# Dense products that read their columns and write their outputs two and two from the halves of a tile

## The chip, the cores and the metric

One core of a Trainium2 chip runs the whole kernel. The metric is the device time of one launch in microseconds; lower is better. TensorE does the matrix products into PSUM (8 banks of 512 fp32 a partition), ScalarE (ACT) and VectorE (DVE) prepare operands and take results out, the SyncE queue (SP) loads from HBM.

## What is computed

One inference step of a decoder layer for 256 prompt tokens and 8 sequences of 8 sample tokens, 320 token columns in all. The reference, cut to what matters here:

```python
h = rms_norm(x, norm_mix_pre[l])
u = h @ w_in[l]                       # 2048 -> 11264: recurrence, attention and gate columns
...
y_hg = o_hg.reshape(b, L, HG_WIDTH) @ w_branch_hg[l]      # 1024 -> 2048
y_da = o_da.reshape(b, L, DA_WIDTH) @ w_branch_da[l]      # 1024 -> 2048
mixed = (jax.nn.sigmoid(g_hg) * y_hg + jax.nn.sigmoid(g_da) * y_da) @ w_out[l]   # 2048 -> 2048
x = x + rms_norm(mixed, norm_mix_post[l])
h = rms_norm(x, norm_ffn_pre[l])
gate, up = jnp.split(h @ w_ffn_up[l], 2, axis=-1)         # 2048 -> 2 * 5632
ffn = (jax.nn.silu(gate) * up) @ w_ffn_down[l]            # 5632 -> 2048
x = x + rms_norm(ffn, norm_ffn_post[l])
```

Between them lie a gated linear recurrence (HGRN2) and differential attention; the sample tokens also attend to a paged cache of 2048 past tokens for each sequence. Everything is float32.

## The kernel before

All activations are kept transposed: 128 features on the partitions, the 320 tokens (T) along the free dimension, contiguous. A weight "granule" is 128 x 1024 floats (512 KB), loaded by the SP queue into one of 12 (later 8) `raw` slots. Each float is split in two parts of the reduced float32 type F32R (written fp32r in the profile): ACT writes the high part `w_hi`, DVE the rest `w_lo`; activations are split in the same way (`x_hi`/`x_lo`, `h2_hi`/`h2_lo`, `m_hi`/`m_lo`, `br_hi`/`br_lo`, `hid_hi`/`hid_lo`). A product is then the sum of three: high by high, low by high and high by low. So a granule is eight 128 x 128 weight blocks, each used in three matmuls of 320 columns: 24 matmuls, each with its own weight load, adding up in PSUM columns 0 to 319 of a bank (`ps[:, bank, 0:T]`).

These "dense products" are written in seven places: `products` (L410 to L412: input projection, branches, output projection, most of the up projection), `half_products` (L421, the first weight set), `pe_last_set` (L1371 to L1373), `up_half` (L1462) and `pe_first_hidden` (L1493 to L1497), `down_granule` (L1818 to L1820) and `down_end` (L1836 to L1838). The program of each engine is an order written out by hand with semaphores between the engines: `granule_used` lets ACT write the next `w_hi`, `hi_ready` and `lo_ready` lead on to DVE and TensorE; nothing is reordered by a scheduler.

Other matmuls stand among them: attention scores of a cache page group (L912: four products of 32 output rows and 512 columns side by side, read as 4 runs of 128), the values (L947, 256 columns), sums of squares in F32R (L932, L933: 320 and 256 columns), transposes and, at the end, the addition of x by an identity in plain float32 (L1850, L1869: 320 columns).

The stages in order: input projection sets, then eight rounds (one head of the recurrence and attention and one sample sequence each, with 16 dense granules), to about 900 us; branches and output projection; up projection from about 1090 us; down projection to the end.

Of the kernel before, what the change touches and what calls it, by code (L numbers as in the profile page):

```python
# [29 lines left out]
T = SEQ + NB * NQ  # L30
# [11 lines left out]
RAW, HALVES = 8, 4  # L42
# [78 lines left out]
def build(nc, xT, ck, cv, st, pt, w_in, w_hg, w_da, w_out, w_up, w_dn, nrm, hgw, lbl, lamv,  # L121
          table, c_ident, c_scan, c_causal, c_own, c_pick, c_hot, c_coef,
          y_T, k_T, v_T, h_p, h_s):
    with ExitStack() as ctx:
# [12 lines left out]
        w_hi = [sb(f"w_hi{j}", [P, 1024], F32R) for j in range(HALVES)]  # L137
        w_lo = [sb(f"w_lo{j}", [P, 1024], F32R) for j in range(HALVES)]
# [15 lines left out]
        ps = ctx.enter_context(nc.psum_tensor("ps", [P, 8, 512], F32))  # L154
# [95 lines left out]
        m_hi = sb("m_hi", [P, KT, T], F32R, at_branch)  # L250
        m_lo = sb("m_lo", [P, KT, T], F32R, at_branch)
# [11 lines left out]
        h2_hi = sb("h2_hi", [P, KT, T], F32R)  # L263
# [130 lines left out]
        def round_lo(dve, r, kind, q):  # L394

            d = 8 * FIRST + 16 * r + (8 if kind == "D" else 0) + q
            split_lo(dve, d, ring_of(r).slot[kind, q], q)

        def products(pe, r, slot, xh, xl, bank, q, nq, free, by_bank=True):

            pe.wait_ge(lo_ready, r + 1)
            wh = w_hi[slot % HALVES][:, :].rearrange("p (c m k) -> p c m k", c=2, m=4)
            wl = w_lo[slot % HALVES][:, :].rearrange("p (c m k) -> p c m k", c=2, m=4)
            for m in range(4):
                if q == 0:
                    free(m)
                out = ps[:, bank + m, 0:T]
                for c in range(2):
                    first, last = q == 0 and c == 0, q == nq - 1 and c == 1
                    pe.matmul(out, wh[:, c, m, :], xh(c), start=first, stop=False)  # L410
                    pe.matmul(out, wl[:, c, m, :], xh(c), start=False, stop=False)  # L411
                    mm = pe.matmul(out, wh[:, c, m, :], xl(c), start=False, stop=last)  # L412
                if by_bank and q == nq - 1 and m < 3:
                    mm.then_inc(set_done, 1)
            mm.then_inc(granule_used, 1)

        def half_products(pe, w, x, bank, first, last):

            for m in range(4):
                for c in range(2):  # L420
                    mm = pe.matmul(ps[:, bank + m, 0:T], w.rearrange("p (c m k) -> p c m k", c=2, m=4)[:, c, m, :], x(c),  # L421
                                   start=first and c == 0, stop=last and c == 1)
                if last and bank == 0 and m < 3:
                    mm.then_inc(set_done, 1)
            return mm
# [933 lines left out]
        def pe_last_set(pe):  # L1359

            s = BLOCKS - 1
            pe_out_set(pe, s, upto=8 - TOGETHER)
            qs = range(8 - TOGETHER, 8)
            pe.wait_ge(lo_ready, R_OUT + 8 * s + 8)
            for m in range(4):
                for q in qs:
                    wh = w_hi[q % HALVES][:, :].rearrange("p (c m k) -> p c m k", c=2, m=4)
                    wl = w_lo[q % HALVES][:, :].rearrange("p (c m k) -> p c m k", c=2, m=4)
                    for c in range(2):
                        k, last = 2 * q + c, q == 7 and c == 1  # L1370
                        pe.matmul(ps[:, m, 0:T], wh[:, c, m, :], m_hi[:, k, :], start=False, stop=False)  # L1371
                        pe.matmul(ps[:, m, 0:T], wl[:, c, m, :], m_hi[:, k, :], start=False, stop=False)
                        mm = pe.matmul(ps[:, m, 0:T], wh[:, c, m, :], m_lo[:, k, :], start=False, stop=last)  # L1373
                    if m == 3:
                        mm.then_inc(granule_used, 1)
                if m < 3:
                    mm.then_inc(set_done, 1)
# [79 lines left out]
        def up_half(pe, w, x, q, part, first, last):  # L1457

            w4 = w.rearrange("p (c m k) -> p c m k", c=2, m=4)
            for m in range(4):  # L1460
                for c in range(2):
                    mm = pe.matmul(ps[:, 4 * part + m, 0:T], w4[:, c, m, :], x[:, 2 * q + c, :],  # L1462
                                   start=first and c == 0, stop=last and c == 1)
            return mm

# [21 lines left out]
        def pe_first_hidden(pe):  # L1487
            pe.wait_ge(lo_ready, R_UP + 1)
            wh, wl = (w[0][:, :].rearrange("p (c m k) -> p c m k", c=2, m=4) for w in (w_hi, w_lo))
            for c in range(2):  # L1490
                pe.wait_ge(e_act.sem, e_act.at(0, "h0" if c else "ha"))
                for m in range(4):
                    pe.matmul(ps[:, m, 0:T], wh[:, c, m, :], h2_hi[:, c, :], start=c == 0, stop=False)  # L1493
                    pe.matmul(ps[:, m, 0:T], wl[:, c, m, :], h2_hi[:, c, :], start=False, stop=False)
                pe.wait_ge(e_vec.sem, e_vec.at(0, "l0" if c else "la"))
                for m in range(4):
                    mm = pe.matmul(ps[:, m, 0:T], wh[:, c, m, :], h2_lo[:, c, :], start=False, stop=False)  # L1497
            mm.then_inc(granule_used, 1)
            for i, (q, part) in enumerate(FIRST_UP):
                if i == 0:  # L1500
                    continue
                if i == 1:
                    pe.wait_ge(e_act.sem, e_act.at(0, "rs"))
                pe.wait_ge(lo_ready, R_UP + i + 1)
                pe.wait_ge(e_act.sem, e_act.at(0, f"h{q}"))
                wh, wl = w_hi[i % HALVES][:, :], w_lo[i % HALVES][:, :]
                up_half(pe, wh, h2_hi, q, part, q == 0, False)
                up_half(pe, wl, h2_hi, q, part, False, False)
                pe.wait_ge(e_vec.sem, e_vec.at(0, f"l{q}"))
                up_half(pe, wh, h2_lo, q, part, False, q == 7).then_inc(granule_used, 1)  # L1510
                if i == GATE_END:

                    pe.wait_ge(e_vec.sem, e_vec.at(0, "sum"))
                    for e in range(2):
                        own = slice(T // 2 * e, T // 2 * e + T // 2)
                        ins = pe.matmul(ps[:, e, T:T + T // 2], ones[:, :], squares[:, 0, own], start=True, stop=True)
                    e_pe2.done(ins, "ss")
# [270 lines left out]
        def pe_rest(pe):  # L1788
# [18 lines left out]
            def down_granule(pas, k, r, slot, use, q):  # L1807
                pe.wait_ge(lo_ready, r + 1)
                wh, wl = w_hi[slot % HALVES], w_lo[slot % HALVES]
                xh, xl = hid_hi[slot % HALVES][:, :], hid_lo[slot % HALVES][:, :]  # L1810
                for m in range(8):
                    if pas and q == 0:
                        pe.wait_ge(g_act.sem, g_act.at(0, f"c{m}"))
                    if not pas and q == 0 and m in (0, 4):
                        pe.wait_ge(f_vec.sem, f_vec.at(HB - 1, "u" if m else "g"))
                    c = slice(P * m, P * m + P)
                    add = dict(start=False, stop=q > 3, skip_group_check=q > 3)
                    pe.matmul(ps[:, m, 0:T], wh[:, c], xh, **dict(add, start=q == 0))  # L1818
                    pe.matmul(ps[:, m, 0:T], wl[:, c], xh, **add)  # L1819
                    ins = pe.matmul(ps[:, m, 0:T], wh[:, c], xl, **dict(add, stop=q >= 3))  # L1820
                    if q == 11 and m < 7:
                        ins.then_inc(down_done, 1)
                ins.then_inc(granule_used, 1)

            def down_end(pas, k, r, slot, use, q):

                if q < 11:
                    return
                pe.wait_ge(lo_ready, r + 1)
                for m in range(8):  # L1830
                    c = slice(P * m, P * m + P)
                    for back in range(MERGED - 1, -1, -1):
                        at = (slot - back) % HALVES
                        xh, xl = hid_hi[at][:, :], hid_lo[at][:, :]
                        add = dict(start=False, stop=True, skip_group_check=True)
                        pe.matmul(ps[:, m, 0:T], w_hi[at][:, c], xh, **add)  # L1836
                        pe.matmul(ps[:, m, 0:T], w_lo[at][:, c], xh, **add)
                        ins = pe.matmul(ps[:, m, 0:T], w_hi[at][:, c], xl, **add)  # L1838
                        if m == 7:
                            ins.then_inc(granule_used, 1)  # L1840
                    if m < 7:
                        ins.then_inc(down_done, 1)
# [349 lines left out]
```

## Time and profile before

| what | value |
|---|---|
| median of 2 runs | 2034.06 us (2033.51 to 2034.61) |
| the profiled execution's own time | 2033.87 us |
| its span, first to last instruction | 2032.3 us |
| TensorE busy | 2022.9 us, 14806 matmuls |
| VectorE / ScalarE busy | 1047.4 / 826.5 us |
| HBM traffic over the span | 219 GB/s |

The span is what the views below divide; 1.6 us of the execution's time lie outside it. A matmul's row begins when it begins to read, and its end is modelled, so rows overlap: the time from one start to the next, or the number of starts in a stretch, tells what a matmul costs. The clock that TensorE is granted is given as a share of 2.4 GHz.

### The profile page before, as it was taken

To read this page: it belongs to the slowest core of one execution; us is meant where nothing else is said; L and a number is where in the kernel's file an instruction comes from. 1 tells how busy PE (TensorE), PEld (TensorE's weight loads), DVE (VectorE), ACT (ScalarE), POOL (GpSimd) and SP (SyncE) were. 2 spreads that over 40 slices of the span, in tenths; PEclk is the share of its full clock that TensorE was granted. 3 is DMA by queue.
4 is the path that set the end of the run, shared out by engine and by line. 5 is a ranking of instruction groups with operands and counts; after the bars stand their busy time and mean duration, and the time that the engine had idled before them with its cause. 6 is when DMAs were issued, how large, how long until landed. Compare 5 with 4: busy or idle time off the path is not lost.

```text
span 2032.3 us, 38356 instructions
## 1 busy us (share of the span) xinstructions
PE 2022.9 (100%) x14806; PEld 1912.6 (94%) x14806; DVE 1047.4 (52%) x1340; ACT 826.5 (41%) x1099; POOL 74.7 (4%) x119
## 2 busy tenths in 40 slices
PE   9999999999999999999999999999999999999999
PEld 9999888888888888899999999999999999999998
DVE  7443555646556465565547644444444445445445
ACT  6333443434435354354345433333333333435344
POOL 1001010000100000000000000000000000000000
PEclk9999999999999999999999999999999999999999
DMA  8767888988889888876544444445444454444441
GB/s 304 163 230 241 301 335 316 357 306 335 336 315 354 314 332 332 328 277 229 172 143 137 152 149 148 141 145 165 145 152 142 141 164 145 148 151 146 155 144 52
DMA packets 123982, 444.13 MB, mean 219 GB/s; under 512 B 14581, under 2 KB 18709, under 8 KB 123856
## 3 DMA queue, kind: packets, MB, share of 16 engines
q1 hardware_dynamic: 112720, 402.31, 55.5%
q0 software_dynamic: 9968, 39.48, 6.5%
q10 hardware_dynamic: 1232, 1.47, 0.2%
q8 instruction: 43, 0.70, 0.1%
q14 instruction: 19, 0.16, 0.0%
HBM read 423.28 MB, written 22.54 MB: 219 GB/s over the span
## 4 chain that ended last, share of the span: by engine, by line
PE 98%; DMA 1%; DVE 1%; ACT 0%; issue 0%; SPq 0%; DVEq 0%
PE ps L410 23%; PE ps L411 22%; PE ps L412 22%; PE ps L1818 5%; PE ps L1820 5%; PE ps L1819 5%; PE ps L912 3%; PE ps L947 3%; PE ps L1462 3%; PE ps L421 1%; PE ps L921 1%; DMA gates<-uT 0%; DMA raw<-w_hg 0%; PE ps L733 0%; PE ps L720 0%; PE ps L481 0%
## 5 line engine op out<-in xcount | busy, mean ns | idle before, releaser
L369 DVE TENSOR_TENSOR w_lo<-raw,w_hi 128x1024 fp32r<-128x1024 f32 x416 | 505.1, 1223 | 539.5 <-ACT w_hi L364 286.7
L410 PE MATMUL ps<-x_hi,w_hi 128*128 128x320 f32 x1472 | 464.4, 316 | 0.0
L411 PE MATMUL ps<-x_hi,w_lo 128*128 128x320 f32 x1472 | 454.8, 309 | 0.0
L364 ACT ACTIVATE w_hi<-raw 128x1024 fp32r<-128x1024 f32 x236 | 247.9, 1062 | 422.5 <-PE ps L412 395.7
L412 PE MATMUL ps<-x_lo,w_hi 128*128 128x320 f32 x1344 | 415.2, 309 | 0.0
L410 PE MATMUL ps<-h_hi,w_hi 128*128 128x320 f32 x1280 | 395.8, 309 | 0.0
L411 PE MATMUL ps<-h_hi,w_lo 128*128 128x320 f32 x1280 | 395.8, 309 | 0.0
L412 PE MATMUL ps<-h_lo,w_hi 128*128 128x320 f32 x1280 | 395.8, 309 | 0.0
L410 PEld LDWEIGHTS ps<-x_hi,w_hi 128*128 128x128 f32 x1472 | 276.5, 188 | 36.1 <-issue 29.2
L411 PEld LDWEIGHTS ps<-x_hi,w_lo 128*128 128x128 f32 x1472 | 276.7, 188 | 0.1
L412 PEld LDWEIGHTS ps<-x_lo,w_hi 128*128 128x128 f32 x1344 | 252.5, 188 | 0.0
L410 PEld LDWEIGHTS ps<-h_hi,w_hi 128*128 128x128 f32 x1280 | 240.4, 188 | 0.0
L411 PEld LDWEIGHTS ps<-h_hi,w_lo 128*128 128x128 f32 x1280 | 240.4, 188 | 0.0
L412 PEld LDWEIGHTS ps<-h_lo,w_hi 128*128 128x128 f32 x1280 | 240.4, 188 | 0.0
L1818 PE MATMUL ps<-hid_hi,w_hi 128*128 128x320 f32 x680 | 210.1, 309 | 0.0
L1820 PE MATMUL ps<-hid_lo,w_hi 128*128 128x320 f32 x680 | 210.0, 309 | 0.0
L1819 PE MATMUL ps<-hid_hi,w_lo 128*128 128x320 f32 x680 | 210.0, 309 | 0.0
L392 ACT ACTIVATE w_hi<-raw 128x1024 fp32r<-128x1024 f32 x124 | 130.0, 1054 | 109.3 <-DMA raw<-w_in 97.1
L1818 PEld LDWEIGHTS ps<-hid_hi,w_hi 128*128 128x128 f32 x680 | 127.7, 188 | 0.1
L1819 PEld LDWEIGHTS ps<-hid_hi,w_lo 128*128 128x128 f32 x680 | 127.7, 188 | 0.0
L1820 PEld LDWEIGHTS ps<-hid_lo,w_hi 128*128 128x128 f32 x680 | 127.7, 188 | 0.0
L1760 DVE TENSOR_TENSOR hid_lo<-hidden,hid_hi 128x320 fp32r<-128x320 f32 x88 | 43.3, 492 | 154.5 <-ACT w_hi L1667 154.1
(330 smaller groups left out, 2375.0 us busy)
## 6 DMA issues: line engine op xcount, KB each, us to landing
raw<-w_in SPq DMA_DIRECT2D x176, 512.0 KB, 6.4
raw<-w_up SPq DMA_DIRECT2D x176, 512.0 KB, 3.5
raw<-ck SPq DMA_DIRECT2D x128, 512.0 KB, 6.2
raw<-cv SPq DMA_DIRECT2D x128, 512.0 KB, 6.9
raw<-w_dn SPq DMA_DIRECT2D x88, 512.0 KB, 3.5
raw<-w_out SPq DMA_DIRECT2D x32, 512.0 KB, 3.7
uT<-stage POOLq DMA_DIRECT2D x14, 640.0 KB, 3.9
raw<-w_hg SPq DMA_DIRECT2D x16, 512.0 KB, 4.6
```

Source lines behind the costliest of these rows:

```text
L364: act.activation(w_hi[slot % HALVES][:, :], raw[slot][:, :], ACT.Copy).then_inc(hi_ready, 1)
L369: dve.tensor_tensor(w_lo[half][:, :], raw[slot][:, :], w_hi[half][:, :].bitcast(F32), ALU.subtract).then_inc(lo_ready, 1)
L392: act.activation(w_hi[q % HALVES][:, :], raw[ring_of(r).slot[kind, q]][:, :], ACT.Copy).then_inc(hi_ready, 1)
L410: pe.matmul(out, wh[:, c, m, :], xh(c), start=first, stop=False)
L411: pe.matmul(out, wl[:, c, m, :], xh(c), start=False, stop=False)
L412: mm = pe.matmul(out, wh[:, c, m, :], xl(c), start=False, stop=last)
L912: ins = pe.matmul(ps[32 * j:32 * j + 32, 7, :], q_rows[:, h, :], raw_all[:, at:at + QUAD, h * PAGE:(h + 1) * PAGE], start=e == 0, stop=e == 1)
L947: ins = pe.matmul(ps[32 * j:32 * j + 32, 6, 0:2 * DV], p_keys[:, p, 32 * j:32 * j + 32], raw[slot][:, 2 * DV * j:2 * DV * (j + 1)], start= ...
L1462: mm = pe.matmul(ps[:, 4 * part + m, 0:T], w4[:, c, m, :], x[:, 2 * q + c, :], start=first and c == 0, stop=last and c == 1)
L1818: pe.matmul(ps[:, m, 0:T], wh[:, c], xh, **dict(add, start=q == 0))
L1819: pe.matmul(ps[:, m, 0:T], wl[:, c], xh, **add)
L1820: ins = pe.matmul(ps[:, m, 0:T], wh[:, c], xl, **dict(add, stop=q >= 3))
```

## The change

A helper `paired` splits the 320 columns of a tile into two halves of 160 and each half into 80 pairs, and walks them in the order: pair 0 of the first half, pair 0 of the second, pair 1 of the first, and so on (columns 0, 1, 160, 161, 2, 3, 162, 163, ...). Every dense product reads its moving operand in this order and writes its PSUM output in the same order, so that each column lands where it did. No tile is stored differently, and the weights are read as before. The built program has as many instructions on each engine as before, in the same order; only the form of these matmuls is now 128x80x2x2 in place of 128x320. The other matmuls are left alone. All lines below the helper move down by 4.

```diff
+        def paired(cols):
+
+            return cols.rearrange("p (a b c) -> p b a c", a=2, c=2)
+
         def products(pe, r, slot, xh, xl, bank, q, nq, free, by_bank=True):
...
-                out = ps[:, bank + m, 0:T]
+                out = paired(ps[:, bank + m, 0:T])
                 for c in range(2):
                     first, last = q == 0 and c == 0, q == nq - 1 and c == 1
-                    pe.matmul(out, wh[:, c, m, :], xh(c), start=first, stop=False)
-                    pe.matmul(out, wl[:, c, m, :], xh(c), start=False, stop=False)
-                    mm = pe.matmul(out, wh[:, c, m, :], xl(c), start=False, stop=last)
+                    pe.matmul(out, wh[:, c, m, :], paired(xh(c)), start=first, stop=False)
+                    pe.matmul(out, wl[:, c, m, :], paired(xh(c)), start=False, stop=False)
+                    mm = pe.matmul(out, wh[:, c, m, :], paired(xl(c)), start=False, stop=last)
...
-                xh, xl = hid_hi[slot % HALVES][:, :], hid_lo[slot % HALVES][:, :]
+                xh, xl = paired(hid_hi[slot % HALVES][:, :]), paired(hid_lo[slot % HALVES][:, :])
...
-                    pe.matmul(ps[:, m, 0:T], wh[:, c], xh, **dict(add, start=q == 0))
-                    pe.matmul(ps[:, m, 0:T], wl[:, c], xh, **add)
-                    ins = pe.matmul(ps[:, m, 0:T], wh[:, c], xl, **dict(add, stop=q >= 3))
+                    pe.matmul(paired(ps[:, m, 0:T]), wh[:, c], xh, **dict(add, start=q == 0))
+                    pe.matmul(paired(ps[:, m, 0:T]), wl[:, c], xh, **add)
+                    ins = pe.matmul(paired(ps[:, m, 0:T]), wh[:, c], xl, **dict(add, stop=q >= 3))
```

The other five places are edited in the same way.

## Rows read from the trace of the kernel before

**Rows 1.** The page: busy time by engine, and the granted clock in 40 slices.

```profile
PE 2022.9 (100%) x14806; PEld 1912.6 (94%) x14806; DVE 1047.4 (52%) x1340; ACT 826.5 (41%) x1099; POOL 74.7 (4%) x119
...
PEclk9999999999999999999999999999999999999999
```

**Rows 2.** The page: the chain that ended last, by engine.

```profile
PE 98%; DMA 1%; DVE 1%; ACT 0%; issue 0%; SPq 0%; DVEq 0%
```

**Rows 3.** Waits of TensorE: us in total, times, longest.

```profile
PE ps L481 <- DVE ones L1956: 1.8, 1, 1.8
PE ps L960 <- ACT o_rows L831: 1.2, 1, 1.2
```

**Rows 4.** The page: loads of the weights by tensor, with their count.

```profile
raw<-w_in SPq DMA_DIRECT2D x176, 512.0 KB, 6.4
raw<-w_up SPq DMA_DIRECT2D x176, 512.0 KB, 3.5
...
raw<-w_dn SPq DMA_DIRECT2D x88, 512.0 KB, 3.5
raw<-w_out SPq DMA_DIRECT2D x32, 512.0 KB, 3.7
...
raw<-w_hg SPq DMA_DIRECT2D x16, 512.0 KB, 4.6
raw<-w_da SPq DMA_DIRECT2D x16, 512.0 KB, 8.4
```

**Rows 5.** Stretches: busy time and starts (x) of each engine, clock, DMA share, GB/s.

```profile
core 0: us, PE busy (x) PEld busy (x) DVE busy (x) ACT busy (x) POOL busy (x), PEclk, DMA share, GB/s
1300.00:1900.00 600.00, 600.00 (x4092) 599.91 (x4091) 277.37 (x261) 215.39 (x246) 0.00 (x0) 1.00 0.45 149
...
100.00:200.00 100.00, 100.00 (x686) 99.93 (x685) 39.67 (x40) 31.51 (x33) 9.39 (x15) 1.00 0.66 226
...
250.00:350.00 100.00, 100.00 (x814) 85.32 (x813) 56.31 (x102) 44.45 (x70) 9.09 (x14) 1.00 0.88 329
```

**Rows 6.** Timeline at 277 us: start us, duration us, instruction.

```profile
277.20 0.30 PE L932 MATMUL ps<-sq_hi,ones_r 128*128 128x320 f32 x1
277.20 0.19 PEld L933 LDWEIGHTS ps<-sq_lo,ones_r 128*128 128x128 f32 x1
277.34 0.31 PE L933 MATMUL ps<-sq_lo,ones_r 128*128 128x320 f32 x1
277.34 0.19 PEld L932 LDWEIGHTS ps<-sq_hi,ones_r 128*128 128x128 f32 x1
277.49 0.28 PE L932 MATMUL ps<-sq_hi,ones_r 128*128 128x256 f32 x1
277.49 0.19 PEld L933 LDWEIGHTS ps<-sq_lo,ones_r 128*128 128x128 f32 x1
277.61 0.28 PE L933 MATMUL ps<-sq_lo,ones_r 128*128 128x256 f32 x1
```

**Rows 7.** Timeline at 2021 us: plain float32 additions by an identity.

```profile
2021.60 2.59 PE L1869 MATMUL ps<-ffn,ident 128*128 128x320 f32 x9
```

**Rows 8.** Timeline at 216 us: page scores, four groups of four matmuls.

```profile
216.40 1.92 PE L912 MATMUL ps<-raw,q_rows 128*32 128x512 f32 x16
```

**Rows 9.** Groups by line and shape: xcount, busy us, mean ns of one.

```profile
L912 PE MATMUL ps<-raw,q_rows 128*32 128x512 f32 x512 | 61.6, 598 | 0.0
...
L1869 PE MATMUL ps<-ffn,ident 128*128 128x320 f32 x18 | 5.3, 432 | 0.0
```

**Rows 10.** The page: the two splits of a weight granule.

```profile
L369 DVE TENSOR_TENSOR w_lo<-raw,w_hi 128x1024 fp32r<-128x1024 f32 x416 | 505.1, 1223 | 539.5 <-ACT w_hi L364 286.7
...
L364 ACT ACTIVATE w_hi<-raw 128x1024 fp32r<-128x1024 f32 x236 | 247.9, 1062 | 422.5 <-PE ps L412 395.7
```

More of the change, by code:

```diff
@@ L420, in half_products @@
                 for c in range(2):
-                    mm = pe.matmul(ps[:, bank + m, 0:T], w.rearrange("p (c m k) -> p c m k", c=2, m=4)[:, c, m, :], x(c),
-                                   start=first and c == 0, stop=last and c == 1)
+                    mm = pe.matmul(paired(ps[:, bank + m, 0:T]), w.rearrange("p (c m k) -> p c m k", c=2, m=4)[:, c, m, :],
+                                   paired(x(c)), start=first and c == 0, stop=last and c == 1)
                 if last and bank == 0 and m < 3:
@@ L1370, in pe_last_set @@
                         k, last = 2 * q + c, q == 7 and c == 1
-                        pe.matmul(ps[:, m, 0:T], wh[:, c, m, :], m_hi[:, k, :], start=False, stop=False)
-                        pe.matmul(ps[:, m, 0:T], wl[:, c, m, :], m_hi[:, k, :], start=False, stop=False)
-                        mm = pe.matmul(ps[:, m, 0:T], wh[:, c, m, :], m_lo[:, k, :], start=False, stop=last)
+                        pe.matmul(paired(ps[:, m, 0:T]), wh[:, c, m, :], paired(m_hi[:, k, :]), start=False, stop=False)
+                        pe.matmul(paired(ps[:, m, 0:T]), wl[:, c, m, :], paired(m_hi[:, k, :]), start=False, stop=False)
+                        mm = pe.matmul(paired(ps[:, m, 0:T]), wh[:, c, m, :], paired(m_lo[:, k, :]), start=False, stop=last)
                     if m == 3:
@@ L1461, in up_half @@
                 for c in range(2):
-                    mm = pe.matmul(ps[:, 4 * part + m, 0:T], w4[:, c, m, :], x[:, 2 * q + c, :],
+                    mm = pe.matmul(paired(ps[:, 4 * part + m, 0:T]), w4[:, c, m, :], paired(x[:, 2 * q + c, :]),
                                    start=first and c == 0, stop=last and c == 1)
@@ L1492, in pe_first_hidden @@
                 for m in range(4):
-                    pe.matmul(ps[:, m, 0:T], wh[:, c, m, :], h2_hi[:, c, :], start=c == 0, stop=False)
-                    pe.matmul(ps[:, m, 0:T], wl[:, c, m, :], h2_hi[:, c, :], start=False, stop=False)
+                    pe.matmul(paired(ps[:, m, 0:T]), wh[:, c, m, :], paired(h2_hi[:, c, :]), start=c == 0, stop=False)
+                    pe.matmul(paired(ps[:, m, 0:T]), wl[:, c, m, :], paired(h2_hi[:, c, :]), start=False, stop=False)
                 pe.wait_ge(e_vec.sem, e_vec.at(0, "l0" if c else "la"))
                 for m in range(4):
-                    mm = pe.matmul(ps[:, m, 0:T], wh[:, c, m, :], h2_lo[:, c, :], start=False, stop=False)
+                    mm = pe.matmul(paired(ps[:, m, 0:T]), wh[:, c, m, :], paired(h2_lo[:, c, :]), start=False, stop=False)
             mm.then_inc(granule_used, 1)
@@ L1833, in down_end @@
                         at = (slot - back) % HALVES
-                        xh, xl = hid_hi[at][:, :], hid_lo[at][:, :]
+                        xh, xl = paired(hid_hi[at][:, :]), paired(hid_lo[at][:, :])
                         add = dict(start=False, stop=True, skip_group_check=True)
-                        pe.matmul(ps[:, m, 0:T], w_hi[at][:, c], xh, **add)
-                        pe.matmul(ps[:, m, 0:T], w_lo[at][:, c], xh, **add)
-                        ins = pe.matmul(ps[:, m, 0:T], w_hi[at][:, c], xl, **add)
+                        pe.matmul(paired(ps[:, m, 0:T]), w_hi[at][:, c], xh, **add)
+                        pe.matmul(paired(ps[:, m, 0:T]), w_lo[at][:, c], xh, **add)
+                        ins = pe.matmul(paired(ps[:, m, 0:T]), w_hi[at][:, c], xl, **add)
                         if m == 7:
```

## The prediction

> **What bounds the kernel now.** I read the page first, from the top. TensorE is busy for 2022.9 of 2032.3 us at the full granted clock, which is 2.4 GHz [rows 1], and the chain that ended last is TensorE for 98% [rows 2]. The view of waits says the same from the other side: the longest waits of TensorE are single ones of 1.8 and 1.2 us [rows 3]. So the kernel is one queue of matmuls, and whatever changes the time of a dense matmul changes the end by that, times the number of them. Since rows of matmuls overlap and their ends are modelled, their durations (0.31 us) say nothing here. I count starts. From 1300 to 1900 us, where nothing but dense products runs, there are 4092 starts in 600 us: 600 / 4092 = 146.6 ns each [rows 5]. This step is the same where the DMA engines are at 0.45 and where they are at 0.66 (686 starts in 100 us, 145.8 ns) [rows 5], so memory traffic does not set it.
>
> **How many there are.** The weights come in 176 + 176 + 88 + 32 + 16 + 16 = 504 granules [rows 4], each of 24 matmuls: 12,096. At 146.6 ns that is 1773 us of the 2032.3 us. All of them are changed; the other 2710 of the 14806 are not.
>
> **What the 146.6 ns are made of.** At 2.4 GHz, 320 columns at one a clock would take 133.3 ns. Two neighbours tell what lies above. The sums of squares at 277 us have the same type: the step from one start to the next is 0.14 to 0.15 us after 320 columns and 0.12 us after 256 [rows 6]. So 64 columns are worth about 0.027 us, close to one a clock (26.7 ns), and the time goes with the columns. Each of these also has its own weight load of 128 columns, and one of them was over in time for a step of 0.12 us; a weight load is not what holds the dense step at 0.147 us. The second neighbour is plain float32 at the end: nine matmuls of 320 columns take 2.59 us from the first start to the last end, one lasts 0.432 us, so a step is (2.59 - 0.432) / 8 = 0.270 us [rows 7, 9]. That is two clocks a column (266.7 ns) and 3.3 ns over. With those 3.3 ns as the cost of beginning a matmul, an F32R one of 320 columns should take 136.6 ns. It takes 10.0 ns more, which no row explains. Twelve thousand times 10.0 ns are 121 us: this is all that a better walk over the columns could win.
>
> **The change part by part.**
>
> Instructions, waits, loads, evacuations: nothing is added, removed or moved; each matmul is still one instruction with one weight load, and its output lands in the same columns, so ACT and DVE read banks as before. Cost 0.
>
> The moving operand is read as pairs of 4-byte elements, 8 bytes, with a jump of 640 bytes forward or back between pairs: 160 pairs and 159 jumps. The trace of before has no matmul that reads so. The nearest rows: the page scores read 512 columns as four runs of 128, with three jumps. Sixteen of them, in four groups of four that run side by side, take 1.92 us to the last end, one lasts 0.598 us [rows 8, 9], so a group's step is (1.92 - 0.598) / 3 = 0.441 us at most, where 512 columns at two clocks and the start cost would be 430 ns. Three jumps cost at most 11 ns together, and probably less, since the four of a group begin a little apart. This excludes an expensive jump, not a cheap one: 159 jumps at 11 / 3 ns would be 583 ns, far more than the other bound. So the bounds are taken thus. From below: the 10.0 ns vanish, -10.0 x 12,096 = -121 us. From above: the columns go at the rate of plain float32, (270 - 146.6) x 12,096 = +1493 us.
>
> The output is written in the same order, 8 bytes to a place. Its bounds are the same two, and it shares them with the read, since both go column by column in one stream.
>
> I take 0 for both. The row that it is nearest to is the dense step itself: at 2.4 GHz one column a clock is a stream that is most easily delivered as two 4-byte elements at a time, and a walk that keeps pairs together asks for as many pairs as before. The steps at 277 us [rows 6], with a slope of one clock a column, fit a stream with no refetch cost that a jump could multiply.
>
> A rule bears on this. The Trainium skill, page "Advanced Engine Details and Errata", section "Memory Cachelines", says that PSUM has lines of two fp32 values, SBUF lines of 16 bytes that want at least two hits each, and that "every two consecutive elements should be contiguous for best throughput": by that the change costs nothing, since each pair fills a PSUM line and hits an SBUF line twice. The same section says that any non-contiguous access pattern significantly slows down matmuls; by that the time would be that of the second rival below. No row of this trace shows either, because no matmul in it hops within 128 columns. The Trainium skill's page "Vector Engine (DVE) Microarchitecture Reference", section "Measured stream behaviour on trn2", gives for VectorE 1.065 ns a column with all streams hopping in aligned pairs against 1.054 contiguous; if TensorE did alike, an estimate is 1% of 1773 us, 18 us, which is inside no change. No run here shows that.
>
> Sum: 2033.87 us (the profiled execution's own time, 0.2 us under the median of 2034.06) + 0 = 2034 us. If it is off by a nanosecond a matmul either way it moves by 12 us, so this case by itself reaches from 2015 to 2060.
>
> **The rivals.**
>
> *The 10 ns go (faster).* If the unexplained 10.0 ns are a clash between neighbouring columns of one tile, say a PSUM column that is read to be added to while the last one is written, taking turns between two halves could separate them. For it: the excess is there in F32R and missing in plain float32, which asks for half as much in a time. Against it: the same clash would show in the slope, and from 256 to 320 columns the slope looks like one clock. Time: 2034 - 121 = 1913 us. The other engines would follow: a granule would take 24 x 136.6 = 3.28 us against 1.223 us of DVE and 1.062 us of ACT for its splits [rows 10]; in the rounds the DMA engines, now at 0.88 [rows 5], would be asked for about 5% more, 0.92.
>
> *Each hop costs a fetch (slower).* If the excess is the price of going from one 16-byte run of four floats to the next, 80 times a matmul, the paired walk does that 160 times and pays it twice: +10.0 ns, or +13.3 ns if the 3.3 ns belong to it too. Time: 2034 + 121 = 2155 to 2034 + 161 = 2195 us. It decides from the first matmul, as nothing hides TensorE. For it: an excess of 10 ns over 80 runs is a plausible 0.13 ns each. Against: again the slope.
>
> *The stream falls to half rate (much slower).* If full rate needs long contiguous runs, in the operand or in PSUM, the dense step becomes that of plain float32, 270 ns: 2034 + 1493 = 3527 us. For it: the trace shows only two rates, and nothing in it shows full rate without contiguity; scores with jumps run at the slower one already, and can't tell. Against: nothing but the pairs themselves.
>
> *The change does nothing*, because the walk is put back in order when built. The form of the instruction in the built program (128x80x2x2) speaks against it; its time is that of the forecast and it is counted there.
>
> **How the numbers follow.** No change 0.50 (2015 to 2060 us); the excess goes, in part or whole, 0.14 (1913 us); each hop costs a fetch 0.15 (2155 to 2195 us); half rate or thereabouts 0.21 (3527 us). The range from 1910 to 2200 us holds the first three, 0.79, and leaves out the last. Two per cent, 41 us or 3.4 ns a dense matmul, is about what a measurement of this kernel can tell from no change. Faster by more than that 0.13, within it 0.51, slower 0.36.
>
> **What would show it.** In the profile after, the count of starts from 1300 to 1900 us decides at once: 4092 for no change, about 4390 for the first rival, 3750 to 3830 for the second, 2220 for the third. In the second and third the weight loads would no longer be busy throughout, the splits of ACT and DVE would stand in longer idle times, and GB/s would fall with them. The steps of L932 and L933 must stay at 0.15 and 0.12 us in every case, and the granted clock at full. The forecast is wrong if TensorE's walk over three dimensions has a price of its own, or if pairs are not the unit in which SBUF or PSUM serve it.

## The result and the profile after

The changed kernel takes 2763.55 us (2 runs, 2763.49 to 2763.61) against 2034.06 us: a ratio of 1.3585, 95% interval 1.3552 to 1.3617. That is 729.5 us more.

The page of the kernel after, busy time by engine, granted clock, and the chain that ended last:

```profile
PE 2753.8 (100%) x14806; PEld 2490.7 (90%) x14806; DVE 1051.8 (38%) x1340; ACT 826.0 (30%) x1099; POOL 74.5 (3%) x119
...
PEclk9999999999999999999999999999999999999999
...
PE 99%; DVE 0%; DMA 0%; ACT 0%; issue 0%; SPq 0%; DVEq 0%
```

The counts and the clock are those of [rows 1, 2], and the work of DVE and ACT is the same to within half a per cent: the same instructions, TensorE hardly ever waiting, and all of the time gone into its matmuls. The stretches of the kernel after show the dense step (columns: stretch, busy time and starts of each engine, clock, DMA share, GB/s):

```profile
1800.00:2400.00 600.00, 600.00 (x2905) 566.13 (x2904) 194.36 (x170) 142.98 (x149) 0.00 (x0) 1.00 0.33 107
```

Against 4092 starts in [rows 5] there are 2905: 600 / 2905 = 206.5 ns a matmul. Times 12,096, the 59.9 ns more are 725 us of the 729.5. The waits of TensorE stay single and small, and the split of a weight granule on DVE takes as long as in [rows 10] with more idle time in front of it (waits, then the group on the page):

```profile
PE ps L485 <- DVE ones L1960: 1.8, 1, 1.8
PE ps L964 <- ACT o_rows L835: 0.6, 1, 0.6
```

```profile
L369 DVE TENSOR_TENSOR w_lo<-raw,w_hi 128x1024 fp32r<-128x1024 f32 x416 | 506.9, 1224 | 866.5 <-ACT w_hi L364 534.3
```

Matmuls that were not changed kept their time. The sums of squares, of the same type and read in plain order in the midst of the slower ones, still step by 0.15 us after 320 columns and 0.12 us after 256, as in [rows 6]. The additions by an identity at the end do too: from 2753.64 to 2754.72 us four records, 0.270 us each, as in [rows 7].

```profile
378.24 0.32 PE L936 MATMUL ps<-sq_hi,ones_r 128*128 128x320 f32 x1
378.39 0.31 PE L937 MATMUL ps<-sq_lo,ones_r 128*128 128x320 f32 x1
378.54 0.28 PE L936 MATMUL ps<-sq_hi,ones_r 128*128 128x256 f32 x1
378.66 0.28 PE L937 MATMUL ps<-sq_lo,ones_r 128*128 128x256 f32 x1
...
2753.64 1.24 PE L1854 MATMUL ps<-o_all,ident 128*128 128x320 f32 x4
2754.72 1.24 PE L1873 MATMUL ps<-ffn,ident 128*128 128x320 f32 x4
```

### The profile page after: what moved, and what is told of

It is laid out like the page before. It is cut to its first block, busy times and chain, and to the rows that moved or that the text cites. A ratio compares the mean times of both kernels' runs of the same rounds, so it can differ in the third digit from the quotient of the medians.

```text
span 2761.9 us, 38356 instructions
## 1 busy us (share of the span) xinstructions
PE 2753.8 (100%) x14806; PEld 2490.7 (90%) x14806; DVE 1051.8 (38%) x1340; ACT 826.0 (30%) x1099; POOL 74.5 (3%) x119
## 4 chain that ended last, share of the span: by engine, by line
PE 99%; DVE 0%; DMA 0%; ACT 0%; issue 0%; SPq 0%; DVEq 0%
PE ps L414 24%; PE ps L415 23%; PE ps L416 23%; PE ps L1824 5%; PE ps L1822 5%; PE ps L1823 5%; PE ps L1466 3%; PE ps L916 2%; PE ps L951 2%; PE ps L425 1%; PE ps L925 1%; PE ps L737 0%; PE ps L724 0%; DVE ffn L1784 0%; PE ps L697 0%; PE ps L674 0%
## 5 line engine op out<-in xcount | busy, mean ns | idle before, releaser
L414 PE MATMUL ps<-x_hi,w_hi 128*128 128x320 f32 x1472 | 566.5, 385 | 0.0
L415 PE MATMUL ps<-x_hi,w_lo 128*128 128x320 f32 x1472 | 558.1, 379 | 0.0
L416 PE MATMUL ps<-x_lo,w_hi 128*128 128x320 f32 x1344 | 509.5, 379 | 0.0
L414 PE MATMUL ps<-h_hi,w_hi 128*128 128x320 f32 x1280 | 492.8, 385 | 0.0
L415 PE MATMUL ps<-h_hi,w_lo 128*128 128x320 f32 x1280 | 492.8, 385 | 0.0
L416 PE MATMUL ps<-h_lo,w_hi 128*128 128x320 f32 x1280 | 492.8, 385 | 0.0
L414 PEld LDWEIGHTS ps<-x_hi,w_hi 128*128 128x128 f32 x1472 | 286.2, 194 | 54.3 <-issue 35.0
L1822 PE MATMUL ps<-hid_hi,w_hi 128*128 128x320 f32 x680 | 261.8, 385 | 0.0
L1823 PE MATMUL ps<-hid_hi,w_lo 128*128 128x320 f32 x680 | 261.8, 385 | 0.0
L1824 PE MATMUL ps<-hid_lo,w_hi 128*128 128x320 f32 x680 | 261.8, 385 | 0.0
```

Of the source, the lines that this page charges most:

```text
L414: pe.matmul(out, wh[:, c, m, :], paired(xh(c)), start=first, stop=False)
L415: pe.matmul(out, wl[:, c, m, :], paired(xh(c)), start=False, stop=False)
L416: mm = pe.matmul(out, wh[:, c, m, :], paired(xl(c)), start=False, stop=last)
L1822: pe.matmul(paired(ps[:, m, 0:T]), wh[:, c], xh, **dict(add, start=q == 0))
L1823: pe.matmul(paired(ps[:, m, 0:T]), wl[:, c], xh, **add)
L1824: ins = pe.matmul(paired(ps[:, m, 0:T]), wh[:, c], xl, **dict(add, stop=q >= 3))
```

## The experiments

### Is it the read or the write?

Two kernels each do one half of the change.

```diff
 # e1_read_pairs: against the kernel after
-                out = paired(ps[:, bank + m, 0:T])
+                out = ps[:, bank + m, 0:T]
...
 # e2_write_pairs: against the kernel after
-                    pe.matmul(out, wh[:, c, m, :], paired(xh(c)), start=first, stop=False)
+                    pe.matmul(out, wh[:, c, m, :], xh(c), start=first, stop=False)
```

> The dense products read their moving columns two and two from the halves, but write their outputs in plain order (the columns of the output are then permuted: the result is not the reference's). The changed kernel takes 2763.6 us, a dense step of 206.5 ns against 146.6. Theory W (PSUM writes in pairs are what costs): the step stays at about 147 ns and the time at 2034 us. Theory R (the operand's reads in pairs cost): 206 ns and about 2763 us. Theory B (each costs and they add up): a step in between, about 176 ns, 2390 us.

> The dense products read their moving columns in plain order and write their outputs two and two to the halves (output columns permuted, not the reference's). Theory W: a step of about 206 ns, 2763 us. Theory R: 147 ns, 2034 us. Theory B: in between, about 176 ns, 2390 us.

Reading alone takes 2766.74 us, writing alone 2033.49 us (one run each), beside 2033.77 us for the kernel before. The stretches, first of e1_read_pairs, then of e2_write_pairs:

```profile
1800.00:2400.00 600.00, 600.00 (x2905) 566.13 (x2904) 197.28 (x171) 142.73 (x149) 0.00 (x0) 1.00 0.31 107
```

```profile
1300.00:1900.00 600.00, 600.00 (x4092) 599.91 (x4092) 277.49 (x261) 215.16 (x247) 0.00 (x0) 1.00 0.44 149
```

The counts of starts are those of after and of before, to the last one. Theory R holds: the whole loss is in the read of the moving operand, and writing PSUM in pairs is free.

### What does a hop cost?

e3_runs4 takes four columns from each half in turn, and does the whole computation.

```diff
-            return cols.rearrange("p (a b c) -> p b a c", a=2, c=2)
+            return cols.rearrange("p (a b c) -> p b a c", a=2, c=4)
```

> The walk takes four columns from each half in turn instead of two (80 runs in place of 160), reads and writes both. If the 60 ns are paid per hop (0.38 ns each), 30 ns remain: step 176.5 ns, about 2399 us. If what costs is leaving a 16-byte run before it is used up, runs of four on 16-byte boundaries cost nothing: step 147 ns, 2034 us. If any pattern of three dimensions goes at the slower rate, 206 ns, 2763 us.

It takes 2112.68 us, 1.0389 of before (1.0372 to 1.0406). The stretch from 1350 to 1950 us:

```profile
1350.00:1950.00 600.00, 600.00 (x3915) 599.98 (x3914) 265.86 (x248) 206.34 (x232) 0.00 (x0) 1.00 0.42 142
```

The step is 600 / 3915 = 153.3 ns, 6.7 above plain. Half the hops cost a ninth of the loss. So the price is not one per hop (176 was expected of that), and nearly all of it goes when a run fills 16 bytes, though not all.

### The walk by itself

e4_probe is the kernel before with sets of 16 extra matmuls behind its last one, each set another walk; what they compute is thrown away.

```python
def walk(cols, a, c):
    return cols.rearrange("p (a b c) -> p b a c", a=a, c=c)
...
for i in range(16):
    pe.matmul(acc(), wt(i), walk(hx[:, 0:T], 2, 1), start=True, stop=True)
```

> The kernel before with 36 sets of extra matmuls behind its last one (16 each, the first 64 to keep the clock up), F32R, 320 columns unless said, output to one bank, each set on a line of its own; only their steps are read, the time is that of before plus some 90 us. Plain order: Theory of a fixed cost: step = N / 2.4 + 13 ns at N = 128 to 512; theory of a cost by column: 0.458 ns x N. Read pairs: 206 ns by theory R, 147 by W; write pairs the other way round. Runs of 4, 8, 16: per hop 176, 161, 154 ns; by 16-byte runs 147 for all. Pairs with jumps of 16 bytes to 1280 bytes: all alike if a hop costs whatever its length; the 16-byte one cheaper if lines of memory are kept. Single columns (read only): about 267 ns if a fetch serves two columns. Pairs from an odd column: slower than even ones if fetches are 8 bytes. Plain float32 in pairs: 270 ns as in plain order if only the full rate is hurt.

Rows of its timeline (start us, us to the last end, line, xcount). A step is the start of the next row less that of this one, divided by 16:

```profile
2036.69 2.51 PE L1888 MATMUL ps<-w_lo,w_hi 128*128 128x320 f32 x16
2039.04 3.62 PE L1890 MATMUL ps<-w_lo,w_hi 128*128 128x320 f32 x16
2042.48 2.51 PE L1892 MATMUL ps<-w_lo,w_hi 128*128 128x320 f32 x16
2044.82 3.59 PE L1894 MATMUL ps<-w_lo,w_hi 128*128 128x320 f32 x16
2048.25 2.62 PE L1896 MATMUL ps<-w_lo,w_hi 128*128 128x320 f32 x16
...
2065.16 2.33 PE L1910 MATMUL ps<-w_lo,w_hi 128*128 128x320 f32 x16
2067.33 3.50 PE L1912 MATMUL ps<-w_lo,w_hi 128*128 128x320 f32 x16
2070.66 4.71 PE L1914 MATMUL ps<-w_lo,w_hi 128*128 128x320 f32 x16
2075.18 4.82 PE L1916 MATMUL ps<-w_lo,w_hi 128*128 128x320 f32 x16
...
2105.04 1.90 PE L1934 MATMUL ps<-w_lo,w_hi 128*128 128x128 f32 x16
2106.78 1.98 PE L1936 MATMUL ps<-w_lo,w_hi 128*128 128x192 f32 x16
2108.59 2.09 PE L1938 MATMUL ps<-w_lo,w_hi 128*128 128x256 f32 x16
2110.52 2.94 PE L1940 MATMUL ps<-w_lo,w_hi 128*128 128x384 f32 x16
2113.30 3.46 PE L1942 MATMUL ps<-w_lo,w_hi 128*128 128x448 f32 x16
2116.60 3.84 PE L1944 MATMUL ps<-w_lo,w_hi 128*128 128x512 f32 x16
```

| walk of e4_probe (320 columns, read unless said) | line | step ns |
|---|---|---|
| plain | L1888 | (2039.04 - 2036.69) / 16 = 146.9 |
| pairs from the halves: read / write / both | L1890, L1892, L1894 | 215 / 146 / 214 |
| runs of 4 from the halves: read / write / both | L1896, L1898, L1900 | 154 / 146 / 153 |
| runs of 8, of 16, both | L1906, L1908 | 153, 151 |
| **single columns from the halves** | L1910 | **(2067.33 - 2065.16) / 16 = 135.6** |
| pairs from the halves, from an odd column | L1912 | 208 |
| pairs from 80, 40, 20, 10, 5 streams | L1914 to L1922 | 271 to 290 |
| the same five, written | L1924 to L1932 | 146 to 150 |
| plain, 128 / 192 / 256 / 384 / 448 / 512 columns | L1934 to L1944 | 109 / 113 / 121 / 174 / 206 / 229 |
| one weight block for all; two banks in turn; adding up | L1946 to L1950 | 146 to 147 |

A step taken so holds the passage from one set to the next, which moves the mean of a set by a few ns beside a set of another rate, and by more beside plain float32: in e8_probe3 256 columns in singles (L1926) come out at 131 ns behind such a set and in e5_probe2 at 113.

Three things stand there. Writes by pairs or longer runs cost next to nothing in any order: eight orders written took 146 to 150 ns. At 128 and 192 columns the step is some 110 ns however few the columns. The load of 128 weight columns, which all of them have, is the likely reason, but no run varied it; at 320 columns the step is above that floor. And reading single columns in turn from the two halves, the one walk that I had held to be worse still (267 ns in the expectation), is 11 ns **faster than plain order**.

### Is that a chance of one tile?

> The kernel before with 50 sets of 16 extra matmuls (after 64 to keep the clock up) behind its last one, outputs in plain order; only their steps are read. In the first such run a read in plain order took a step of 146.6 ns, pairs from the halves 216, pairs with jumps of 16 to 256 bytes 271 to 290, single columns from the halves 135.8. Theory L (what costs is that reads close together in time fall on the same part of memory, and two streams far apart avoid it): singles stay at 136 for every distance of the two streams but a few that are multiples of a large power of two, whatever the tile and its offset; four or eight streams also 136. Theory S (135.8 is a chance of that one tile and distance): the steps scatter between 136 and 290 with distance, offset and tile. Read with a step of two columns in one stream: 136 by L if neighbours clash, 146 or more if whole lines count. By count of columns, singles: N / 2.4 + 2.5 ns for 256 and up; 112 ns below, where the weight load is the longer. If the weight load were what disturbs the plain read, one and the same weight block would give another step than two in turn (it gave 146.6 both).

Rows of its timeline: L1890 is the first of eleven sets of single columns from two streams 160 to 511 columns apart, L1912 the first of eight of pairs, at 160 to 320.

```profile
2039.11 2.33 PE L1890 MATMUL ps<-w_lo,w_hi 128*128 128x320 f32 x16
...
2063.02 3.58 PE L1912 MATMUL ps<-w_lo,w_hi 128*128 128x320 f32 x16
...
2089.53 2.59 PE L1928 MATMUL ps<-w_lo,w_hi 128*128 128x320 f32 x16
...
2126.64 4.70 PE L1960 MATMUL ps<-w_lo,w_hi 128*128 128x320 f32 x16
2131.15 4.71 PE L1962 MATMUL ps<-w_lo,w_hi 128*128 128x320 f32 x16
2135.68 2.91 PE L1964 MATMUL ps<-w_lo,w_hi 128*128 128x320 f32 x16
2138.43 4.54 PE L1966 MATMUL ps<-w_lo,w_hi 128*128 128x320 f32 x16
```

The eleven sets: (2063.02 - 2039.11) / 176 = 135.9 ns each, whatever the distance; the eight of pairs (2089.53 - 2063.02) / 128 = 207 ns. Singles begun at columns 1, 2, 4, 8 and 64, and on two other tiles, are at 136 too (plain: 146 to 148 there, 152 from column 1). One stream with a step of two columns takes (2131.15 - 2126.64) / 16 = 282 ns, four streams of single columns 172 ns, eight 272 ns. By count, singles take 163 ns for 384 columns, 189 for 448 and 216 for 512: one clock of 2.4 GHz a column and 2 to 3 ns. So theory S falls, and so does theory L, by which four and eight streams should have been at 136.

Plain float32 behaves otherwise: a record takes 269 ns in plain order (e4_probe L1952), (9.13 - 0.441) / 31 = 280 ns in pairs (L1954) and (11.00 - 0.502) / 31 = 339 ns in singles (e5_probe2 L1986), each from the first start to the last end less one record. These sets show something that I had missed in [rows 7, 9]: 16 plain float32 matmuls stand in the trace as x32. One is two records, 538 ns in all, so my upper bound took half of such a matmul for a whole one. It was no bound either: read in single columns from sixteen streams, an F32R matmul takes 311 ns (e5_probe2 L1968).

### The gain on the whole kernel

e7_read_singles changes the read alone (outputs are then permuted); e6_singles does the whole computation, and keeps the split tiles so that the reads come in the natural order of tokens (in one place two DVE instructions become four).

```diff
 # e6_singles: against the kernel before
+        def in_turn(kept):
+
+            return kept.rearrange("p (a b) -> p b a", a=2)
+
+        def kept_as(tile):
+
+            return tile.rearrange("p (a b) -> p a b", a=2) if len(tile.shape) == 2 else tile.rearrange("p n (a b) -> p n a b", a=2)
+
+        def split_of(tokens):
+
+            return tokens.rearrange("p (b a) -> p a b", a=2) if len(tokens.shape) == 2 else tokens.rearrange("p n (b a) -> p n a b", a=2)
...
-                    pe.matmul(out, wh[:, c, m, :], xh(c), start=first, stop=False)
+                    pe.matmul(out, wh[:, c, m, :], in_turn(xh(c)), start=first, stop=False)
...
-                    ins = act.activation(x_hi[:, g, :], x_raw[:, g, :], ACT.Copy, scale=nrm_w[:, 0, g:g + 1])
+                    ins = act.activation(kept_as(x_hi[:, g, :]), split_of(x_raw[:, g, :]), ACT.Copy, scale=nrm_w[:, 0, g:g + 1])
```

> All dense products of the kernel read their columns one and one from the halves (0, 160, 1, 161, ...), tiles stored as they are, outputs written in plain order (so the output columns are permuted, not the reference's). If the 135.8 ns of the extra matmuls hold for every operand tile, the step falls by 10.8 ns, 12,096 times: 131 us, 1903 us, unless the loads of the rounds or the splits become the bound, which would leave some 1930 to 1960 us. If it was a chance of that tile: between 2034 and 2760 us, with steps that differ by tile.

> The whole computation with that read: each split operand tile is kept with its even tokens in the first half and its odd tokens in the second (the ACT and DVE instructions that write high and low parts read their source with a step of two columns), and the dense products read one and one from the halves, so that they see the tokens in their natural order and write plain outputs. If the readers of e7 gain, this gains as much, 1903 us, less what slower ACT and DVE writers add where they lie on the path: at most the first set and the start of the up projection, some 5 to 10 us. If reading with a step of two slowed ACT or DVE by half in the down projection (one activation and one subtraction of 320 columns a granule, 0.5 us each), a granule would still need under 2.5 us of 3.26 us, and nothing is lost.

e7_read_singles takes 1906.62 us (0.9372 of before, 0.9357 to 0.9388), e6_singles 1906.84 us (0.9375, 0.9359 to 0.9391), beside 2033.99 us. The stretches of e6_singles, up projection and a round, and one of its groups:

```profile
1250.00:1850.00 600.00, 600.00 (x4418) 599.80 (x4417) 298.84 (x295) 239.53 (x281) 0.00 (x0) 1.00 0.47 160
250.00:350.00 100.00, 100.00 (x922) 82.84 (x921) 54.50 (x91) 43.31 (x68) 6.35 (x10) 1.00 0.91 343
```

```profile
L1680 ACT ACTIVATE hid_hi<-hidden 128x320 fp32r x72 | 36.6, 509 | 126.4 <-PE ps L1834 126.4
```

The step is 600 / 4418 = 135.8 ns; (146.6 - 135.8) x 12,096 = 131 us, of which 127 came out. In the round the DMA engines went from 0.88 [rows 5] to 0.91 and did not stop it. ACT's high part of the hidden tile, now with a step of two columns in its source, takes 509 ns where it took 472 in the kernel before, beside a granule of 24 x 135.8 = 3.26 us; e6_singles is no slower for it than e7_read_singles. TensorE now waits for a weight split, as it never did in the kernel before, 0.9 us in all:

```profile
PE ps L422 <- DVE w_lo L369: 0.9, 3, 0.3
```

### What the walk has to keep

> The kernel before with 22 more sets of 16 extra matmuls behind its last one, outputs plain; only their steps are read. Known so far (320 columns, F32R): plain 146.6 ns; two streams read column by column in turn 135.8 at every distance from 160 columns up; four such streams 170, eight 273; one stream with a step of two or three columns 283; pairs in turn from two streams 206 to 217, from five or more 271 to 290. Theory D (it is the distance of two successive reads that counts, near ones clash): two streams at 2, 4 or 8 columns inside a block read slower than 136 and only far ones reach it; the same column twice in turn, and one column 320 times, would be the worst. Theory T (each of two alternating read slots fetches ahead for its own stream and holds a piece of it, so two streams are served well wherever they are, and fetches count by the fresh pieces that they need): 135.8 at all distances from 8 columns up; two streams each with a step of two columns waste half of each piece and go to some 200 to 280; the same column twice is at 136 or less. Runs of 16, 32 and 80 from the halves: 151, 149 and 147 (towards plain). Pairs from four streams are slower than from two (206), runs of four from four streams about like from two (153) by a cost per 16-byte piece.

Rows of its timeline: L1890 reads two streams 2 columns apart in turn (0, 2, 1, 3, 4, 6, ...), L1892 to L1900 4, 8, 16, 32 and 80 columns apart, L1902 each of 160 columns twice, L1904 one column 320 times, L1906 two streams each with a step of two columns:

```profile
2038.81 2.51 PE L1890 MATMUL ps<-w_lo,w_hi 128*128 128x320 f32 x16
2041.16 2.33 PE L1892 MATMUL ps<-w_lo,w_hi 128*128 128x320 f32 x16
...
2052.02 2.34 PE L1902 MATMUL ps<-w_lo,w_hi 128*128 128x320 f32 x16
2054.20 2.38 PE L1904 MATMUL ps<-w_lo,w_hi 128*128 128x320 f32 x16
2056.41 2.50 PE L1906 MATMUL ps<-w_lo,w_hi 128*128 128x320 f32 x16
2058.75 2.61 PE L1908 MATMUL ps<-w_lo,w_hi 128*128 128x320 f32 x16
...
2073.60 2.46 PE L1918 MATMUL ps<-w_lo,w_hi 128*128 128x320 f32 x16
2075.90 2.63 PE L1920 MATMUL ps<-w_lo,w_hi 128*128 128x320 f32 x16
```

At 2 columns apart the step is 146.9 ns, from 4 up (2052.02 - 2041.16) / 80 = 135.8, each column twice 136, one column 138, two streams with a step of two 146. Theory D (near reads clash) falls: the nearest reads of all are among the fastest. Theory T fell too where it gave two spaced streams 200 to 280 ns. The other sets of the run: read in runs of 16, 32 and 80 from the halves 153, 149 and 147 ns; pairs from four streams 274 ns; runs of four from four streams (L1918) (2075.90 - 2073.60) / 16 = 144 ns, less than plain order, where about the 153 of two streams was expected, and from eight streams 154 ns.

A third one, theory P, fits most of them, and the next run tries it on walks not yet seen. It does not fit walks in which one of its readers goes back and forth between pieces that it has begun: by its rule pairs from the two halves and single columns from four streams should both take 283 ns, and they took 207 and 172.

> The kernel before with 11 more sets of 16 extra matmuls behind its last one, outputs plain; only their steps are read. Theory P, made from the sets so far: the reads of a matmul go by turns to two readers, the first takes reads 1, 3, 5, ..., the second 2, 4, 6, ..., and what counts is how many reads in a row a reader makes in one aligned piece of four columns (16 bytes): 4 or more, 135.8 ns; 2, 146.7 ns; 1, 283 ns (0.885 ns a column). Rival C (a piece costs by how often the walk as a whole goes to another one: 80 times in plain order, 320 in turns). The sets: two streams with a step of 3 columns: P 1.33 a piece, about 220 ns; with a step of 4 columns, 256 of them: P 227 ns. One stream with a step of 2, 256 columns: 227 ns by both. Every second column read twice: P 146.7. Every fourth column read twice: P 283, C about 200 (160 pieces, as pairs). Two pieces in turn column by column, then two left out: P 135.8. Runs of four from the halves, but from column 2 on, so that each run lies on two pieces: P 1 read a piece and reader, 206 to 283, against 153 when aligned. Runs of eight from column 2: P about 180 to 210. Runs of four, the second stream one column off: P between 153 and 283, since one of the readers crosses pieces.

Its timeline:

```profile
2041.42 3.58 PE L1892 MATMUL ps<-w_lo,w_hi 128*128 128x320 f32 x16
2044.83 3.85 PE L1894 MATMUL ps<-w_lo,w_hi 128*128 128x256 f32 x16
2048.50 3.86 PE L1896 MATMUL ps<-w_lo,w_hi 128*128 128x256 f32 x16
2052.18 2.52 PE L1898 MATMUL ps<-w_lo,w_hi 128*128 128x320 f32 x16
2054.54 4.73 PE L1900 MATMUL ps<-w_lo,w_hi 128*128 128x320 f32 x16
2059.09 2.36 PE L1902 MATMUL ps<-w_lo,w_hi 128*128 128x320 f32 x16
2061.29 3.51 PE L1904 MATMUL ps<-w_lo,w_hi 128*128 128x320 f32 x16
2064.63 3.68 PE L1906 MATMUL ps<-w_lo,w_hi 128*128 128x320 f32 x16
2068.14 3.47 PE L1908 MATMUL ps<-w_lo,w_hi 128*128 128x320 f32 x16
```

| walk | line | P | measured ns |
|---|---|---|---|
| two streams, step 3 | L1892 | 220 | 213 |
| two streams, step 4, 256 columns | L1894 | 227 | 229 |
| one stream, step 2, 256 columns | L1896 | 227 | 230 |
| every second column twice | L1898 | 146.7 | 147.5 |
| every fourth column twice | L1900 | 283 (rival C: 200) | 284 |
| two pieces in turn, two left out | L1902 | 135.8 | 137.5 |
| runs of 4 from column 2 | L1904 | 206 to 283 | 209 |
| runs of 8 from column 2 | L1906 | 180 to 210 | 219 |
| runs of 4, second stream one column off | L1908 | 153 to 283 | 206 |

The six sets for which P gave one number came within 4% of it, and rival C is out by 84 ns on the one that told the two apart. Of the three for which P gave only a range, two of them wide, two fell inside and the third is 9 ns above.

## Why the prediction was wrong

**The bound** was right: TensorE alone sets the end, and 12,096 times the change of a step gave 725 of 729.5 us. So were the unchanged rest, and the cover of the other engines.

**The step that failed** is "I take 0 for both", and in it the reason that "a walk that keeps pairs together asks for as many pairs as before". For the write it holds: e2_write_pairs stayed at 146.6 ns a step. For the read it does not: its term is 59.9 ns a matmul, 725 us, in place of 0. The unit is not a pair of neighbours in time. By theory P the odd reads and the even reads go two ways, and each way wants to stay in one aligned piece of four columns. In plain order each makes two reads a piece (0 and 2; 1 and 3), to which P puts down the 10 ns over one clock a column. In the paired walk one of them reads 0, 160, 2, 162 and the other 1, 161, 3, 163: each read is in another piece than the one before. The pairs, whole in time, are torn apart on both ways. What the runs show of this without the theory: pairs kept whole in the same two places took 206.5 ns where single columns took 135.8 and aligned runs of four 153, so a pair is not what the read is served by; and one stream with a step of two columns took 282 ns where two such streams in turn, with as many pieces and two reads in each, took 146. The size of the loss P does not give: its rule says 283 ns for the paired walk. A cost between the two rates was not among my cases: between the second rival's 2195 us and the third's 3527 us I had put nothing. The prediction's last sentence did name two signs of its being wrong. A walk over three dimensions with a price of its own is not it: writing by one is free, and reading by one in runs of four costs 6.7 ns. Pairs not being the unit in which SBUF serves the read is.

**The lower bound** of -121 us was a true size for a thing that this change does not do: the 10 ns can go, 127 us of them did in e6_singles, by a walk that is the changed one with runs of one in place of two (135.8 ns, where the prediction had 136.6 for a matmul without them). My first rival looked for their cause in PSUM; e7_read_singles, which changes the read alone and takes 1906.62 us, puts it in the read.

**The argument from the slope** misled me. I read one clock a column off a single step of 0.12 us at 256 columns [rows 6] and concluded that there was no cost by the piece. The extra sets give 121 ns at 256 columns and 229 at 512, 0.42 ns a column, against (216 - 163) / 128 = 0.41 for singles from 384 to 512. But plain order does not go by one line: the difference between the two walks is 8 ns at 256 columns, 9 at 288, 11 at 320 and 384, 17 at 448 and 13 at 512. It grows with the columns, unevenly, and a single step read to 10 ns, at 256 columns near the floor of some 110 ns, could not show that. It hid a mechanism that changes with the walk, and only changing the walk could show it.

**The second rival** (each hop to another run of 16 bytes costs a fetch) had the right sign. It counts 80 hops for plain order, 160 for the paired walk and 80 again for the runs of four of e3_runs4, which lost only 6.7 ns. Its price was wrong: 10.0 to 13.3 ns for the 80 more, where 59.9 were lost. And so was its count, by the walk as a whole: single columns from the halves go to another run 320 times and are the fastest walk of all, at 135.8 ns.

**The rule of the Trainium skill** that I weighed, page "Advanced Engine Details and Errata", section "Memory Cachelines": in PSUM two consecutive elements contiguous for best throughput, in SBUF at least two hits on a line of 16 bytes. The measurement decides against the second as a promise of full speed for F32R reads: pairs on 16-byte lines took 206.5 ns, plain order 146.6, and 135.8 came with single columns in turn, by P four reads on a line by each way. What it says of 16 bytes agrees with the runs of four that lost all but 6.7 ns when aligned (153) and fell back to 209 when begun two columns later. Its sentence that non-contiguous patterns slow matmuls is, for PSUM writes, not borne out: eight orders of writing in pairs or runs took 146 to 150 ns.

**What stays open.** That the loss lies in the read, and that it depends on the order of the columns within 16-byte pieces, is shown. Theory P is a model that fits most of the sets; no row shows two readers. It does not say why alternating between two pieces costs less than going on to ever new ones (pairs from two halves 207 ns, from four streams 274, single columns from four streams 172), which looks as if an earlier piece were kept for a while. So it does not give the 206.5 ns of this change. Nor is that step quite fixed: the same walk took 215 ns in e4_probe and 213 in e5_probe2 (L1912). That aligned runs of 4 and 8 from the halves cost 6 ns more than plain order is not explained, nor that runs of 4 from four streams cost 3 ns less, nor the 280 and 339 ns of plain float32. Writes of single columns in turn weren't tried.

## What to carry to other kernels

Where a stream of F32R matmuls of 320 columns or so is what sets the end, and its step is some 10 ns over the columns at one a clock, read the moving operand one and one from two places at least four columns apart, such as its two halves (every distance tried from 4 to 511 columns gave 136 ns), and let the instruction that writes the operand store it so that this is the natural order: here 146.6 to 135.8 ns a matmul and 6.25% of the kernel, with writers on ACT some 8% slower. At 288 to 512 columns the extra sets gained 9 to 17 ns; no whole kernel was tried there. Read patterns need a measurement of their own before they are called free; sixteen extra matmuls of each pattern behind the kernel's last one give the steps of thirty patterns in one run, to a few ns. In a matmul's output a walk by aligned pairs cost nothing in any order tried.

## What the runs showed of the hardware

- The rate of reading a moving F32R operand depends on the order of its columns by more than a factor of two: 320 columns in 135.8 ns (two streams, one and one), 146.6 (plain), 153 (aligned runs of 4 from the halves), 207 (pairs from the halves), 282 (one stream with a step of two) and 311 (sixteen streams), at the full clock of 2.4 GHz throughout.
- 135.8 ns is 320 columns at one a clock (133.3) and 2.5 ns.
- With 256 columns or fewer in that order the step stays at 108 to 113 ns. The load of 128 weight columns is the likely floor, which no run isolated; the better walk wins 8 ns at 256 columns (121 to 113).
- A plain float32 matmul stands in the trace as two records of 269 ns.
